# Gate projection of a decoder trunk as seven block products, with the per-layer rows kept in DRAM and the tail in halves

## What is computed

```python
h = h + f.astype(h.dtype)                                   # f: ConvGLU feed-forward, its last product is @ w_down
gate = jax.nn.sigmoid(rmsnorm(h, norm_ple_w[i]) @ w_pg[i])  # w_pg: 2048 x 2048
h = h + ((p[i] @ w_ple[i]) * gate).astype(h.dtype)          # w_ple: 256 x 2048
return rmsnorm(h, final_norm_w)
```

## Time and profile before

| | us |
|---|---|
| median of 3 runs | 2189.91 (2189.76 to 2190.01) |
| the profiled execution, its own time | 2189.98 |
| its span in the trace | 2188.6 |
| last down product ends | 1970.0 |
| gate stage on PE | 1992.5 to 2166.5 |
| tail, to the end of the span | 22.1 |

### The profile page before, as it was taken

One profiled execution on the slowest core, in us unless ns is written; L12 is line 12 of the kernel. 1 busy time (PEld: TensorE's weight loads), 2 busy tenths in 40 slices (PEclk: granted clock), 3 DMA queues, 4 the chain that ended last, 5 costly groups with the idle time before them and its releaser, 6 DMA issues.

```text
span 2188.6 us, 28780 instructions
## 1 busy us (share of the span) xinstructions
PE 2168.0 (99%) x10788; PEld 1833.1 (84%) x10788; DVE 1380.8 (63%) x1719; ACT 885.0 (40%) x1024; POOL 305.0 (14%) x329
## 2 busy tenths in 40 slices
PE   9999999999999999999999999999999999999997
PEld 7888878888888888888888888888888888888886
DVE  7486336453378988888888888886334333346444
ACT  6223246442243554445454455544222122226443
POOL 6993004000000111111111111110000000000001
PEclk9999999999999999999999999999999999999999
DMA  6422322134332777777777777766343332232222
GB/s 222 135 75 95 103 97 82 58 121 168 120 118 103 217 208 211 204 201 188 205 213 204 207 190 197 211 200 242 104 137 107 127 123 93 95 121 106 96 96 77
DMA packets 106037, 321.53 MB, mean 147 GB/s; under 512 B 8224, under 2 KB 56992, under 8 KB 85760
## 3 DMA queue, kind: packets, MB, share of 16 engines
q1 hardware_dynamic: 76256, 268.39, 34.3%
q0 software_dynamic: 29728, 52.44, 13.0%
HBM read 298.77 MB, written 22.02 MB: 147 GB/s over the span
## 4 chain that ended last, share of the span: by engine, by line
PE 96%; ACT 1%; DVE 1%; DMA 0%; SPq 0%; issue 0%; DVEq 0%; ACTq 0%
PE bank L1012 23%; PE bank L682 19%; PE bank L684 19%; PE bank L683 19%; PE bank L1014 12%; PE bank L796 1%; ACT xs_hi L1118 1%; DMA Y<-in_x 0%; PE bank L756 0%; PE bank L781 0%; PE bank L769 0%; PE bank L866 0%; DVE Y L2177 0%; PE bank L868 0%; PE bank L853 0%; DVE w_lo L1540 0%
## 5 line engine op out<-in xcount | busy, mean ns | idle before, releaser
L1012 PE MATMUL bank<-x_block,w_hi 128*128 128x512 f32 x2240 | 777.4, 391 | 1.2 <-DVE w_lo L1947 1.2
L1014 PE MATMUL bank<-x_block,w_lo 128*128 128x256 f32 x2240 | 629.0, 281 | 0.0
L1094 ACT ACTIVATE w_hi<-w_raw 128x2048 fp32r<-128x2048 f32 (+1 forms) x134 | 222.4, 1660 | 734.0 <-PE bank L684 721.2
L1012 PEld LDWEIGHTS bank<-x_block,w_hi 128*128 128x128 f32 x2240 | 419.6, 187 | 92.6 <-DVE w_lo L1947 1.5
L1014 PEld LDWEIGHTS bank<-x_block,w_lo 128*128 128x128 f32 x2240 | 423.3, 189 | 0.0
L682 PE MATMUL bank<-xs_hi,w_hi 128*128 128x512 f32 x1024 | 404.9, 395 | 3.8 <-DVE xs_lo L1564 2.8
L684 PE MATMUL bank<-xs_hi,w_lo 128*128 128x512 f32 x1024 | 398.8, 389 | 0.0
L683 PE MATMUL bank<-xs_lo,w_hi 128*128 128x512 f32 x1024 | 398.7, 389 | 0.0
L1540 DVE TENSOR_TENSOR w_lo<-w_raw,w_hi 128x2048 fp32r<-128x2048 f32 (+1 forms) x136 | 272.3, 2002 | 134.2 <-ACT w_hi L1094 131.6
L1395 ACT ACTIVATE w_hi<-Y 128x1024 fp32r<-128x1024 f32 x159 | 168.7, 1061 | 179.9 <-PE bank L1014 125.2
L682 PEld LDWEIGHTS bank<-xs_hi,w_hi 128*128 128x128 f32 x1024 | 192.3, 188 | 48.0 <-issue 6.2
(11 more groups left out here) (348 smaller groups left out, 2502.2 us busy)
## 6 DMA issues: line engine op xcount, KB each, us to landing
w_raw<-in_w_up SPq DMA_DIRECT2D x48, 1024.0 KB, 4.8
w_raw<-in_w_down SPq DMA_DIRECT2D x64, 704.0 KB, 4.1
Y<-in_w_up SPq DMA_DIRECT2D x40, 1024.0 KB, 5.7
w_raw<-in_w_in SPq DMA_DIRECT2D x31, 1024.0 KB, 4.8
Y<-in_w_up POOLq DMA_DIRECT2D x59, 512.0 KB, 6.8
Y<-in_w_up SPq DMA_DIRECT2D x39, 512.0 KB, 7.6
w_raw<-in_w_out SPq DMA_DIRECT2D x16, 1024.0 KB, 5.2
w_raw<-in_w_pg SPq DMA_DIRECT2D x16, 1024.0 KB, 4.7
```

Of the source, the lines that this page charges most:

```text
L1012: nc.tensor.matmul(place(c, b, 0, 2), w_h[:, ks], xb[b][:, k, :, :].rearrange("p e t -> p (e t)"), start=fresh and k == 0, stop=False, ski ...
L1014: last = nc.tensor.matmul(place(c, b), w_l[:, ks], xb[b][:, k, 0, :], start=False, stop=k == HALF_K - 1, skip_group_check=True)
L1094: nc.scalar.activation(w_hi[c % 2][:, 0:width], w_raw[c % 2][:, 0:width], ACT.Copy).then_inc(hi_made, 1)
```

## The change

The gate projection gets the same seven products, 8 pairs of tiles (`GATES`), each product 8 blocks deep with three 256-column matmuls a block (`product` on `gb`, not the joined 512-column matmul). The activation blocks `gb` are made from h: ACT scales rows i and i+8 in place, DVE makes sums of them, ACT and DVE split them. Four blocks (A11, S1, S3, S2) are made row by row during the last down quarter, whose tiles come in the order 0, 8, 1, 9, ... (`last_row`); three (A12, A22, S4) at once, later. Since h is overwritten by this, it is stored to DRAM first (`park_h`) and loaded again. The PLE rows go through DRAM too: ACT copies each into one of six slots, SP stores it and loads it again when its gate is ready. The raw weights of one pair fill both `w_raw` buffers. Sums of squares are added up by DMA. `rstd` is now made in the narrow way (four columns, then spread). The last gate tile is finished in two halves of 256 tokens, and the final spread in quarters.

```diff
+GATES = KT // 2
+EARLY = [A11, S1, S3, S2]
+LATE = [A12, A22, S4]
...
         @block.sync
...
+            def gate_raw_in(c, b):
+                if c == 0:
+                    sp.wait_ge(lo_made, PLE0 + (1 if b in (S3, A22) else 2))
+                elif b == A11:
+                    sp.wait_ge(blk_lo, gate_index(c - 1, S1) + 1)
+                elif b == S3:
+                    sp.wait_ge(g_sums, G_SUMS + 3 * c)
+                else:
+                    sp.wait_ge(blk_lo, gate_index(c - 1, {A22: A22, A12: S4}[b]) + 1)
+                part = slice(BLOCK, 2 * BLOCK) if b in (A12, A22) else slice(0, BLOCK)
+                sp.dma_start(gate_raw(b), A["w_pg"][2 * c + (b in (S3, A22))][:, part]).then_inc(raw_in[b], 16)
...
+            sp.wait_ge(gb_lo, GB_LO + PRODUCTS * HALF_K - 3 * (HALF_K - 1))
+            for c in range(GATES):
+                two = slice(2 * c, 2 * c + 2)
+                sp.dma_start(Y[:, two, :], h_dram[:, two, :]).then_inc(h_back, 16)
+            for c in range(GATES):
+                if c:
+                    ple_row_in(2 * c - 1)
+                if c < GATES - 1:
+                    gate_raw_in(c + 1, A11)
+                if c:
+                    ple_row_in(2 * c)
+                if c < GATES - 1:
+                    for b in (S3, A22, A12):
+                        gate_raw_in(c + 1, b)
...
         @block.tensor
...
-            with pe.Fori(0, KT // 2) as i:
-                for s in range(2):
-                    pe.wait_ge(lo_made, 2 * i + (PG0 + s + 1))
-                    pe.wait_ge(evacuated, 2 * i + (PG0 - 2 + s - 1))
-                    before = (lambda k: pe.wait_ge(xs_lo_made, 3 * KT + k + 1)) if s == 0 else None
-                    tile((PG0 + s) % 2, bank[(PG0 + s) % 2][:], xs_hi, xs_lo, KT, before)
+            def gate_pair(c):
+                for b in range(PRODUCTS):
+                    pe.wait_ge(blk_lo, gate_index(c, b) + 1)
+                    if c == 0:
+                        pe.wait_ge(gb_lo, GB_LO + 4 * HALF_K + (LATE.index(b) + 1 if b in LATE else 0))
+                        if b == 0:
+                            pe.wait_ge(ple_out, KT)
...
+                    if b == A12:
+                        pe.wait_ge(u2_made, FAST + c + 1)
...
+                    for k in range(HALF_K):
+                        ks = slice(k * P, (k + 1) * P)
+                        last = product(place(FAST + c, b), w_h[:, ks], w_l[:, ks], gb[b][:, k, 0, :], gb[b][:, k, 1, :],
+                                       fresh and k == 0, k == HALF_K - 1, onto=True)
+                    last.then_inc(product_done, 1)
...
         @block.vector
...
+            for c in range(GATES):
+                if c:
+                    gate_c12(c - 1)
+                    gate_rest(c, S1)
+                gate_rest(c, A12)
+                if c:
+                    finish_gate(c - 1)
+                gate_s4(c)
+                gate_rest(c, A22)
+                gate_u(c)
+                if c == 0:
+                    dve.wait_ge(rstd_made, 3)
+                gate_rest(c, S4)
+                gate_c22(c)
+                if c < GATES - 1:
+                    gate_rest(c + 1, A11)
+                    gate_rest(c + 1, S3)
+                    gate_sums(c + 1)
+                gate_c11(c)
+                gate_c21(c)
+                if c < GATES - 1:
+                    gate_rest(c + 1, S2)
                 else:
-                    y, g = Y[:, bass.ds(j, 1), :], ple[:, bass.ds(j, 1), :]
-                    v, gate = val[:].unsqueeze(1), conv_acc[:].unsqueeze(1)
...
+                    finish_last(0)
+                finish_value(c)
...
         @block.gpsimd
...
+            def gate_add_in(c):
+
+                pool.wait_ge(raw_in[S3], RAW_IN + 16 * (c + 1))
+                pool.wait_ge(s3_made, 16 * (FAST + c - 1))
+                pool.dma_start(gate_raw(S3), A["w_pg"][2 * c][:, 0:BLOCK], accum_op=ALU.add).then_inc(s3_made, 16)
...
+            gate_add_in(0)
+            gate_add_in(1)
+            for c in range(GATES - 1):
+                add_squares(2 * c, value_sq, c_value)
+                add_squares(2 * c + 1, gate_sq, c_gate)
+                if c + 2 < GATES:
+                    gate_add_in(c + 2)
```

More of the change, by code:

```diff
@@ L1073, in _ @@
+            for _ in range(WARM_GATE):
+                nc.tensor.matmul(bank[4][:, 0:P], ones[:], ident[:], start=True, stop=True)
+            for j in range(4):
+                if j % 2 == 0:
+                    pe.wait_ge(gate_sq, GATE_SQ + GATES + j // 2)
+                m = nc.tensor.matmul(sums[:, j:j + 1], c_gate[:, j * P:(j + 1) * P], ones[:, 0:1], start=False, stop=j == 3,
                                      skip_group_check=True)
```

501 lines of the change are left out of this document (397 added, 104 removed).

## The result

The changed kernel takes 2242.36 us (median of 4 runs, 2242.22 to 2242.86) where the kernel before takes 2189.93 on the same chip: 1.0239 times as long, with a 95% interval of 1.0226 to 1.0252. The prediction said 2217, with 2200 to 2233 as its range. The direction and the mechanism were right, the size was not: the loss is 52.4 us and not 27.6.

The account below looks back on a forecast made before the run. PE bounds the kernel before; after the change the gate's S3 load cycle would, at 23.8 us a pair. Gate end plus 28.6 and tail minus 1.0 give 27.6 on 2189.9: 2217 us, 8-in-10 range 2200 to 2233.

Parts of the forecast that it names:

- T + 64.9: First pair: the rest of S2 of pair 1, counted from T = 1970.0 us, the last down product; 7.6 us later through the reload.
- Products of 256 columns, 0.120 us: Gate matmuls on PE: 0.120 us each, 20.2 us a pair against 21.7 before, a gain of 12.5 if PE never waits.
- the rival of the weight load: Gate matmuls: weight loads pace 256-column products at 0.173 us each, 29.1 us a pair, 2256 us in all; chance 0.06.
- The cycle as the bound: Gate pairs after the first: S3's reuse chain (14.7 + 4.2 + 4.9) sets 23.8 us a pair, above PE's 20.2.
- S3's plain load, 512 KB ... 4.2: Gate cycle: the raw S3 load takes 3.7 us alone, 4.2 beside the load adding squares; ends 2.3 and 4.7.
- the adding load ... 4.9: Gate cycle: POOL's load that adds onto raw S3 takes 4.9 us, priced as alone; ends 4.5 and 6.8.
- The reload, T + 52.3 for raw S3: First pair: eight loads of h ahead of pair 1's weights land raw S3 at T + 52.3 instead of about T + 44.8.
- The handover, 7.3 us: Between down and gate: PE waits for PLE copies, 4.7 us for row 0; gate at T + 29.8, not T + 22.5; ends 3 and 10.
- PLE rows through DRAM at nothing: Gate stage: PLE rows and squares through DRAM cost PE nothing, 3.7 us of DVE work covering some 3.
- Tail, minus 1.0: After the last gate product: final spread in quarters served first, tail 1.0 us shorter; ends 0 to minus 2.
- taken half together: Forecast's own spread: ends of cycle (-13.8, +14.4), handover (-4, +3) and reload (-7.6), half together, give 2203 to 2232.
- cycle is covered: Rival for the gate stage: loads are hidden and PE bounds it, 2185.5 us, or 2178 with a free handover; chance 0.12.

Follow-up runs that it names:

- the filler run: Changed kernel plus unread products on PE, 36 in its wait at the handover and 10 behind the last gate product: 2244.32 us.
- the last kernels: Changed kernel with POOL adding raw A11 to S3 and the S4 sum ahead of `finish_gate` (2211.43 us), and the versions built on it, down to 2195.90 us.
- the kernel of 2200.35 us: Changed kernel with POOL adding raw A11 to S3, the S4 sum ahead of `finish_gate`, and h reloaded two row tiles a pair: 2200.35 us.
- the best version: Kernel of 2200.35 us with S1 sum on POOL, pair 0's addition by DMA, 21 filler products at the handover, 10 at the tail, no `WARM_GATE`: 2195.90 us, ratio 1.0026.

## Why the prediction was wrong in its size

The sum was T + 64.9 for the end of the S2 rest of pair 1, six periods of 23.8, 17.4 for the last pair, and a tail shorter by 1.0. Measured, from the same end: T + 70.1, six of 26.58, 17.65, and a tail longer by 1.95. The miss of 25 us is 5.2 + 16.7 + 0.2 + 3.0.

- **Products of 256 columns, 0.120 us:** right. 0.12 between starts, 20.2 us a pair; the rival of the weight load is out. The Trainium skill ("TensorE: Matmul & The Clock Gate", Back-to-back issue gap) says that load and product together set the spacing. The trace has as many weight loads as products in the stage (1346), and the spacing stayed at 0.12, so no load stretched it to the rival's 0.173.
- **The cycle as the bound, DVE's part 14.4 us:** right. 14.42 measured. That the whole period is 23.71 us once the neighbours are taken away, where 23.8 stood, is partly luck: 3.95 stands there for the 4.5 up to POOL's issue, and 5.35 for the adding load's 4.9.
- **"S3's plain load, 512 KB ... 4.2" and "the adding load ... 4.9":** these two terms failed. With the answers of SP and POOL (0.3) the first is 5.27 and not 4.5, the second 6.89 and not 4.9; together 2.8 a pair and 16.7 in all, two thirds of the miss. The prediction priced the adding load as alone, and forgot that SP issues A22 and A12, 1.05 MB, 1.1 and 3.6 us behind S3: while POOL waits for S3, they fill the engines. Of the adding load's 2.0 us too much the neighbours are 1.3 to 1.5; the other 0.5 is the load itself, 5.35 and not 4.9 even nearly alone. The row with the answer was there: 6.8 us, the upper end, from a load into the same kind of place beside others. I chose the lower end by the 3.0 us that the bytes take; the nearest row in circumstances was the other one. With the upper ends of the prediction's own rows (4.7 and 6.8) the pair came to 26.2, near the 26.58. And the neighbour of the first load, the squares, takes 1.0 to 1.3 where 0.5 was allowed. The Trainium skill ("DMA: Bandwidth & Descriptors", Anatomy of one DMA) has a formula for DMAs that GpSimd issues, from which I estimate 3.2 us for 512 KB. SP's plain load, nearly alone, took 3.5, near it; POOL's adding load took 5.3, so the formula does not hold for one that adds.
- **The reload, T + 52.3 for raw S3:** right in mechanism, 5 us short. The rest of block S4 came at T + 40.1 and not T + 38.0, because its half waited for the store of a PLE row. Then POOL was released 17.3 us after that, not 14.3: again because the loads behind share. By 2028 us all 6.29 MB, h and all four blocks, had moved; I had counted the 5.24 up to S3. Spreading the reload gave 10.7 us, where the term was 7.6.
- **The handover, 7.3 us:** the wait of 4.7 was right (4.82), the start 1.8 late, since the lower clock behind that wait was not in the sum. It stretched the products by 2.4 us (2.9 by the filler run).
- **PLE rows through DRAM at nothing:** right for the rows of the cycle (2.9 us each, no wait of DVE for them); not for the stores at the handover, above.
- **Tail, minus 1.0:** wrong in sign. The prediction looked at the end of the tail and not at its start, where `WARM_GATE` and two more sets of sums stand ahead of the last square's. From the last gate product to the last sums it is 6.9 us, where it was 4.0; from there to the end it is 17.3, where it was 18.3, which is the minus 1.0 of the prediction. `WARM_GATE` itself is in both kernels; what is new is that nothing covers it. With a filler and without these products the first stretch is 4.1 us, and the tail 22.5.
- **The small sums:** 52.3 + 4.9 + 7.5 is 64.7 and not 64.9, and 174.0 less 161.3 is 12.7 and not 12.5. The ends "taken half together" give 2205 to 2226 and not 2203 to 2232. All upper ends together give 2236, still under the measured time.

The rival "cycle is covered" was not reached by any run: it wanted a cycle of about PE's 20.2 us, and the shortest period measured is 21.16. In the last kernels POOL's addition and DVE's rest of S4, side by side, are part of what holds it there. An estimate from the kernel of 2200.35 us: 4.0 us from the S4 sum to POOL, 2.4 for the addition alone, and 13.2 from ACT's half to the next S4 sum in the cycles without a late rest give 19.6, under PE's 20.2. Six periods shorter by 1.2 us would bring the best version to about 2189, the time of the kernel before. An order that keeps these two operations apart was not tried, nor a second place for raw S3, for which I found no room in memory.

## What to carry to other kernels

When a wait on a transfer becomes the bound, price the transfer with everything that is in the queue beside it at that moment, what is issued right behind it too: loads issued one after the other don't land one after the other, they share. If a buffer has to be read before it can be filled again, the load, what is done on arrival and the whole work up to the read add up to one ring, and the mean busy shares of the engines say nothing on it; the ring has to be taken apart at each of its steps. And a load that adds on arrival is worth its slowness only where it is hidden: on the ring, POOL did the same in a third of the time. But look at what runs beside an operation before it goes to POOL: here DVE stood still for up to 2.4 us of each addition, and the trace shows that as busy time.
